# The second layer's attention and expert queries in halves of 256 tokens, with expert gathers interleaved into the second half

## The chip, the cores and the metric

The kernel runs on one core of one Trainium2 chip. The metric is the device time of one execution in microseconds (us). The core has the engines TensorE (PE; its weight loads are shown as PEld), VectorE (DVE), ScalarE (ACT), GpSimd (POOL) and SyncE (SP, which here issues weight loads and result stores), and 16 DMA engines between HBM and SBUF. Each engine runs its own instructions in program order, and the engines meet only at semaphores.

## The reference, cut to what matters

Two transformer layers over 512 tokens of width 1024, all in float32. The first layer (adaptive norm, sparse attention, latent attention, a feed-forward of width 4096) is untouched by the change. The second layer is:

```python
mod = jax.nn.silu(c) @ ada_w[l] + ada_b[l]
h = rmsnorm_2(x, norm1_g[l]) * (1.0 + sc1) + sh1
p = h @ w_in[l]
mq, mk, mv, mo, mi, mf, dq, dk, dv = jnp.split(p, split_pts, axis=-1)
qk = jax.nn.silu(causal_dwconv(jnp.concatenate([mq, mk], axis=-1), conv_w[l], conv_b[l]))
...
hm = mlstm_chunkwise(q_m, k_m, v_m, ig, lf)          # 4 heads of 128
hm = rmsnorm_2(hm, ...) * jax.nn.sigmoid(mo)
...
od = diff_attention(q_d, k_d, v_d, lam)              # 4 heads, two softmaxes each
y = jnp.concatenate([hm, od], axis=-1) @ w_out[l]
x = x + g1 * y
h2 = rmsnorm_2(x, norm2_g[l]) * (1.0 + sc2) + sh2
x = x + g2 * peer(h2, peer_w_query[l], peer_sub_keys[l], peer_u[l], peer_v[l])
return rmsnorm_2(x, final_g)
```

and the experts of it, for each block of 128 tokens:

```python
q = (xb @ w_query).reshape(TOKEN_BLOCK, P_HEADS, 2, P_HALF)
s = jnp.einsum('thpk,hpnk->thpn', q, sub_keys)
sv, si = lax.top_k(s, P_TOPK)                        # 16 of 128 keys, for each half of the key
...
fv, fpos = lax.top_k(cand, P_TOPK)                   # 16 of the 256 pairs
eidx = jnp.take_along_axis(cidx, fpos, axis=-1)
g = jax.nn.softmax(fv, axis=-1)
act = jax.nn.gelu(jnp.einsum('td,thkd->thk', xb, u_tab[eidx]), approximate=False)
return jnp.einsum('thk,thkd->td', g * act, v_tab[eidx])
```

Everything is causal in the tokens: the attention of tokens 0 to 255 needs nothing of tokens 256 to 511.

## The kernel before

Activations are kept transposed: 8 blocks of 128 features by 512 tokens (`xT`, and `hT` for the normed ones). Weights stream through two ring buffers of 2 MB each (`ring`), which SP fills: block n waits until the matmuls of block n-2 are done. A **chunk** is 128 output features, 8 accumulated matmuls of 512 tokens; PE writes it into PSUM bank j % 2, and ACT or DVE evacuates it.

The second layer runs in stages over all 512 tokens: norm `n1`; `in2a`, 17 chunks (the convolved queries and keys, the gates, values and output gates, with the four-tap convolution on DVE, L1392 and L1394); `mls`, the mLSTM attention; `dif`, the differential attention; the output projection `out2`; norm `n2`; the expert queries. The attention classes hand one **unit** (one head of one tile of 128 queries) from PE to DVE to ACT and back in a pipeline of some ten steps. A hook, `fill_pe` and `fill_dve`, puts other work into each step: the 12 chunks of `in2b` go into `mls`, half of `out2` goes into `dif`.

The expert stage has 512 **picks**: pick n is one expert slot (of 16 in each of 8 heads) for a tile of 128 tokens. One pick is

- POOL: an indirect DMA that gathers 128 rows of 8 KB, u and v of an expert for each token, into a row buffer (L1596);
- DVE: the dot product with u (L1513, `dot`);
- ACT: Gelu (L1230) and the scaling by the gate (L1231), and for an odd pick from 16 on also a diagonal matrix of the weights (L1237);
- the product with v: on DVE for even picks (L1525, `value`), on PE by that diagonal matrix for odd ones (L1072).

DVE adds the value of pick n - lag after the dot of pick n. The row buffers are the slots: 4 for the first 32 picks (lag 1), 8 after that (lag 3; four of them lie in `ring`, which is free once the weights are through). A gather waits until the slot's last value is added. Between the picks DVE chooses the experts of later heads: `pick_keys` (L1455 to L1467), `pick_pairs` (L1474 to L1479), `pick_experts` (L1485 to L1495) and `pick_gates`. The queries of tokens 0 to 255 (`pqa`) come ahead of the picks and beside the first ten; those of tokens 256 to 511 (`pqb`) are computed beside picks 10 to 30. Of each tile the sum is then scaled, added to x and normed (`last`, five steps) and stored.

## Time and profile before

| | us |
|---|---|
| median of 3 runs | 2956.39 (2953.14 to 2956.84) |
| the profiled execution, its time | 2954.73 |
| its span in the trace | 2952.6 |
| second layer's first norm (`n1`) begins | 1136.3 |
| first expert gather is issued | 1559.2 |
| eight slots in use | from 1712.8 |
| last dot product begins | 2938.3 |

PE was busy for 2285.1 us, DVE for 1711.7, ACT for 774.1 and POOL for 618.6 of the span. Busy time is that of the instructions themselves. In a row of the timeline, the bracket at the end tells how long the engine sat idle before it, and what ended that. A float32 matmul stands as two records in the trace, so a chunk of 8 matmuls has 16. The indirect DMAs move 1.05 MB each.

### The profile page before, as it was taken

The page shows a single profiled execution, that of the slowest core. Times are in us where ns is not written, and L with a number is a line of the kernel's source. Part 1 is how long each engine was busy: PE and PEld are TensorE (multiplying, and loading weights), DVE is VectorE, ACT ScalarE, POOL GpSimd, SP SyncE. Part 2 cuts the span into 40 slices and gives each one's busy share as a digit, 9 for nine tenths or more (in the row PEclk, how much of TensorE's full clock was granted, in tenths as well). Part 3 has the DMA queues.
Part 4 walks back from the last instruction along what each step waited for, and adds up shares of the span by engine and source line. Part 5 has one row for each costly group of instructions (what it writes and reads, how often), then busy time and mean ns, then how long its engine had stood idle before and what let it go on. Part 6 is the DMA issues. An engine that isn't in the chain of part 4 may idle for free.

```text
span 2952.6 us, 20335 instructions
## 1 busy us (share of the span) xinstructions
PE 2285.1 (77%) x6246; PEld 1108.0 (38%) x6246; DVE 1711.7 (58%) x3473; ACT 774.1 (26%) x2136; POOL 618.6 (21%) x540
## 2 busy tenths in 40 slices
PE   4999999999999999999977755556655565555655
PEld 2475554643444445445546621212212121121221
DVE  5422226312114324223427579999999988999987
ACT  2012332301000002222412223333333333333332
POOL 0000000000000000000002244444445444444443
PEclk8989999999999999999988977676776787768667
DMA  8520002012126520211027799999999999999997
GB/s 347 206 97 29 29 29 86 29 57 81 61 85 250 205 114 33 110 57 57 1 96 295 299 367 418 415 403 406 409 420 418 396 406 410 414 400 418 421 413 333
DMA packets 86070, 702.93 MB, mean 238 GB/s; under 512 B 9552, under 2 KB 9552, under 8 KB 10576
## 3 DMA queue, kind: packets, MB, share of 16 engines
q0 software_dynamic: 77184, 587.24, 48.9%
q1 hardware_dynamic: 7776, 106.96, 9.5%
q10 hardware_dynamic: 1008, 7.52, 0.6%
q8 instruction: 46, 0.75, 0.1%
q14 instruction: 56, 0.46, 0.0%
HBM read 699.58 MB, written 2.10 MB: 238 GB/s over the span
## 4 chain that ended last, share of the span: by engine, by line
PE 50%; DMA 22%; DVE 19%; issue 5%; POOL 2%; ACT 1%; POOLq 0%; ACTq 0%; DVEq 0%
PE PS L396 22%; DMA ring<-in_peer_uv,arena 16%; PE PS L426 8%; DMA arena<-in_peer_uv,arena 5%; DVE arena L1525 5%; PE PS L762 4%; PE PS L462 3%; DVE arena L1513 3%; PE PS L484 3%; PE PS L785 3%; DVE ring L1513 2%; PE PS L472 2%; POOL ring L1596 2%; PE PS L809 2%; PE PS L1072 1%
## 5 line engine op out<-in xcount | busy, mean ns | idle before, releaser
L1072 PE MATMUL PS<-arena 128*128 128x512 f32 x512 | 398.9, 925 | 391.3 <-ACT arena L1237 353.7
L1596 POOL DMA_INDIRECT arena<-in_peer_uv,arena x272 | 319.8, 1176 | 997.3 <-DVE arena L1495 513.3
L1072 PE MATMUL PS<-ring,arena 128*128 128x512 f32 x480 | 318.6, 804 | 156.4 <-ACT arena L1237 156.2
L1513 DVE CUSTOM_DVE_ANT_0 arena<-arena 128x1024 f32<-128x1024 f32 x272 | 327.1, 1223 | 86.3 <-DMA arena<-in_peer_uv,arena 80.8
L396 PE MATMUL PS<-arena,ring 128*128 128x512 f32 x832 | 366.0, 598 | 8.9 <-DVE arena L1322 4.8
L1072 PEld LDWEIGHTS PS<-arena 128*128 128x128 f32 x512 | 128.6, 276 | 631.8 <-ACT arena L1237 513.7
L1596 POOL DMA_INDIRECT ring<-in_peer_uv,arena x240 | 285.7, 1190 | 280.6 <-DVE arena L1525 242.7
L1513 DVE CUSTOM_DVE_ANT_0 ring<-ring,arena 128x1024 f32<-128x1024 f32 x240 | 290.6, 1228 | 48.2 <-DMA ring<-in_peer_uv,arena 47.3
L1230 ACT ACTIVATE arena<-arena 128x1 f32<-128x1 f32 x512 | 102.9, 201 | 808.3 <-DVE arena L1513 807.9
L396 PE MATMUL PS<-hT,ring 128*128 128x256 f32 (+1 forms) x944 | 308.4, 486 | 7.9 <-ACT hT L319 7.9
L1072 PEld LDWEIGHTS PS<-ring,arena 128*128 128x128 f32 x480 | 115.1, 256 | 370.4 <-ACT arena L1237 253.1
L396 PEld LDWEIGHTS PS<-arena,ring 128*128 128x128 f32 x832 | 158.4, 192 | 212.5 <-issue 195.6
L1584 POOL DMA_DIRECT2D arena<-in_ada x24 | 12.9, 539 | 1032.5 <-ACTq L292 762.2
L396 PEld LDWEIGHTS PS<-hT,ring 128*128 128x128 f32 x944 | 181.4, 194 | 127.5 <-issue 111.8
L426 PE MATMUL PS<-hT,ring 128*128 128x512 f32 x512 | 221.8, 596 | 6.5 <-ACT hT L319 6.5
L1525 DVE SCALAR_TENSOR_TENSOR arena<-arena 128x1024 f32<-128x1024 f32 x140 | 179.8, 1284 | 29.2 <-ACT arena L1231 29.2
L1231 ACT ACTIVATE arena<-arena 128x1 f32<-128x1 f32 x512 | 150.8, 295 | 16.6
L1525 DVE SCALAR_TENSOR_TENSOR arena<-ring,arena 128x1024 f32<-128x1024 f32 x120 | 154.1, 1284 | 0.1
L426 PEld LDWEIGHTS PS<-hT,ring 128*128 128x128 f32 x512 | 98.0, 192 | 130.4 <-issue 129.1
L1354 DVE SCALAR_TENSOR_TENSOR xT<-PS,modc,xT 128x512 f32<-128x512 f32 x24 | 18.0, 751 | 218.7 <-PE PS L396 218.7
L1368 DVE TENSOR_SCALAR arena<-PS 128x512 f32<-128x512 f32 x32 | 22.1, 692 | 195.7 <-PE PS L426 195.7
L566 ACT ACTIVATE arena<-arena,smalls 128x128 f32<-128x128 f32 (+3 forms) x128 | 71.7, 560 | 204.3 <-DVE smalls L564 204.3
(252 smaller groups left out, 2550.4 us busy)
## 6 DMA issues: line engine op xcount, KB each, us to landing
ring<-in_wstream SPq DMA_DIRECT2D x50, 2048.0 KB, 7.4
arena<-in_ada POOLq DMA_DIRECT2D x24, 2048.0 KB, 7.9
arena<-in_peer_uv,arena POOLq DMA_INDIRECT x272
ring<-in_peer_uv,arena POOLq DMA_INDIRECT x240, 10.1
xT<-in_xT ACTq DMA_DIRECT2D x1, 2048.0 KB, 11.3
arena<-in_alibi ACTq DMA_DIRECT2D x1, 2048.0 KB, 8.2
result<-arena SPq DMA_DIRECT2D x4, 512.0 KB, 8.0
arena<-in_subkeys ACTq DMA_DIRECT2D x1, 1024.0 KB, 4.9
```

The source lines that it names most:

```text
L396: ins = pe.matmul(o, l, r, start=(a == 0), stop=(a == len(lhs) - 1))
L426: ins = pe.matmul(bank(j % 2, n), w[:, k, m * P:(m + 1) * P], act_in(k), start=(k == 0), stop=(k == kc - 1))
L462: ins = pe.matmul(o, l, r, start=True, stop=True)
L484: ins = pe.matmul(o, l, r, start=(a == 0), stop=(a == len(pairs) - 1))
L762: ins = pe.matmul(bank(7), w[:, k, tile(j % 4)], hT[:, k, :], start=(k == 0), stop=(k == KD - 1))
L785: ins = pe.matmul(bank(5 + j % 2), lhs, rhs, start=(k == 0), stop=(k == KD - 1))
L1072: ins = pe.matmul(bank(6 + b), diag[:, k % NDIAG, :], rows[slot_of(n)][:, D + b * 512:D + (b + 1) * 512], start=opens, stop=closes)
L1230: own(act.activation(dots[:, e:e + 1], dots[:, e:e + 1], ACT.Gelu))
L1231: act.activation(wexp[:, t, e:e + 1], dots[:, e:e + 1], ACT.Copy, scale=gate[:, t, e:e + 1]).then_inc(wexp_ok, 1)
L1513: dve.tensor_tensor_reduce(u, u, h2tok[:, t % 2, :], 1.0, 0.0, ALU.mult, ALU.add, dots[:, e:e + 1]).then_inc(dot_ok, 1)
L1525: dve.scalar_tensor_tensor(out=a, in0=v, scalar=wexp[:, t, e:e + 1], in1=a, op0=ALU.mult, op1=ALU.add)\
L1596: pool.indirect_dma_start(rows[j], None, ap["peer_uv"], bass.IndirectOffsetOnAxis(ap=eidx[:, t, e:e + 1], axis=0)).then_inc(landed[j], 16)
```

## The change

- The second layer's stages run twice, as half a = 0 (tokens 0 to 255) and half a = 1 (tokens 256 to 511). Chunks have 256 columns; a weight block holds two chunks and is 1 MB (`wsecond`, 27 blocks). All 27 are loaded twice, once for each half. `in2b` and `out2` are stages of their own and no longer fill the attention's steps. The fences between the second layer's stages give way to semaphores. Convolution tails, the scans' carries, and the differential attention's keys and values of the first half are carried over; the last go through HBM (`park_kv`), and x, turned to tokens, too (`park_x`, read back when a tile is finished).
- A table of planned step times, `STAGES2`, gives for every step j of a stage the number of picks that must be done before it: `picks(a, stage, j)`. In half 0 that is up to 8, in the query stage `pq` alone. In half 1 it is 8 + 0.62 times the planned microseconds, at most 212. DVE, ACT and PE all bring their part of the picks up to that number (`Feed.to`) ahead of the same step.
- Slots: 4 for the first 16 picks (lag 1), 6 up to pick 272 (lag 2), 8 after that (lag 3).
- `pick_keys` runs once a pick over the first 14 picks of each half, for the heads 2 to 15 of it.

```diff
-EARLY = 32
-NDIAG = 4
+NDIAG = 3
+NARROW, WIDE = 16, NPICK // 2 + 16

 def slot_of(n):
-    return n % 4 if n < EARLY else n % 8
+    if n < NARROW:
+        return n % 4
+    return (n - NARROW) % 6 if n < WIDE else (n - WIDE) % 8

 def lag_of(n):
-    return 1 if n < EARLY else 3
+    return 1 if n < NARROW else 2 if n < WIDE else 3
...
+STAGES2 = [("n1", 1, 10.0), ("in2a", 17, 3.6), ("mls", 18, 2.5), ("in2b", 12, 3.6), ("dif", 26, 2.2), ("out2", 8, 3.6),
+           ("n2", 1, 14.0), ("pq", 20, 3.6), ("park", 1, 4.0)]
+EARLY_PICKS, LAST_PICK, PER_US = 8, 212, 0.62
+
+def picks(a, stage, j):
+    if a == 0:
+        return max(0, min(j - 9, (j - 5) // 2, EARLY_PICKS)) if stage == "pq" else 0
+    start = 0.0
+    for name, steps, us in STAGES2:
+        if name == stage:
+            return min(EARLY_PICKS + int(PER_US * (start + us * j)), LAST_PICK)
+        start += steps * us
...
@@ tensor
+                if a == 1:
+                    pe.wait_ge(x_parked, 32)
+                norm_pe(pe, n1, KD)
...
+                for j in range(17):
+                    values.to(picks(a, "in2a", j))
+                    if 9 <= j < 13:
+                        tokens(IN2A + j)
                     else:
+                        features(IN2A + j, h2T, (lambda k: normed(pe, n1, k)) if j == 0 else None)
...
+                mls[a].fill_pe = lambda pe, u: values.to(picks(a, "mls", u))
+                mls[a].pe(pe)
+                for j in range(12):
+                    values.to(picks(a, "in2b", j))
+                    (features(IN2B + j, h2T) if j < 8 else tokens(IN2B + j))
...
+                dif[a].fill_pe = lambda pe, u: values.to(picks(a, "dif", u))
+                dif[a].pe(pe)
+                pe.wait_ge(dif[a].tok_out, 2)
+                for j in range(8):
+                    values.to(picks(a, "out2", j))
+                    features(OUT2 + j, catT)
+                    norm_after(pe, n2, j)
...
@@ vector
+                for c in range(8):
+                    steps.to(picks(a, "in2a", c))
+                    u, dst = uT[:, c % 4, :], qhalf[:, c, :] if c < 4 else kall[:, c - 4, half(a)]
...
+                    dve.wait_ge(ev2, first + IN2A + c + 1)
...
+                steps.to(picks(a, "in2a", 12))
...
+                mls[a].fill_dve = lambda dve, u: steps.to(picks(a, "mls", u))
+                mls[a].dve(dve, own)
+                for j in range(12):
+                    steps.to(picks(a, "in2b", j))
+                dif[a].fill_dve = lambda dve, u: steps.to(picks(a, "dif", u))
+                dif[a].dve(dve, own)
+                for j in range(8):
+                    steps.to(picks(a, "out2", j))
+                    dve.wait_ge(mm2, first + OUT2 + j + 1)
+                    dve.scalar_tensor_tensor(out=xT[:, j, half(a)], in0=bank((first + OUT2 + j) % 2, HALF),
...
+                for j in range(20):
+                    steps.to(picks(a, "pq", j))
...
@@ scalar, in Attention.act and in the stages
+                    if self.fill_act is not None:
+                        self.fill_act(act, u)
...
+                for tl in range(2):
+                    act.wait_ge(x_pe, 2 * a + tl + 1)
+                    own(act.activation(xtok[:, tl, :]...))
+                    act.dma_start(park_x[2 * a + tl], xtok[:, tl, :]).then_inc(x_parked, 16)
```

How the order of work moves, at two places.

**PE in `in2a`.** Before, chunk after chunk, with nothing but the evacuation of the chunk before last to wait for (L396 is a chunk's matmul):

```order
L396 MATMUL PS<-hT,ring0 128x512 [waits evac]
L396 MATMUL PS<-hT,ring0 128x512 x7
L396 MATMUL PS<-hT,ring0 128x512 [waits evac]
L396 MATMUL PS<-hT,ring0 128x512 x7
L396 MATMUL PS<-hT,ring1 128x512 [waits evac,w_loaded1]
L396 MATMUL PS<-hT,ring1 128x512 x7
```

Now, in half 1 (L1050 is the value of an odd pick, L1080 a chunk's matmul; `diagonals` is ACT's diagonal matrix of that pick):

```order
L1050 MATMUL PS<-whole 128x512 [waits diagonals]
L1050 MATMUL PS<-whole 128x512
L1080 MATMUL PS<-whole 128x256 [waits mm2_taken,w2_loaded1]
L1080 MATMUL PS<-whole 128x256 x7
L1050 MATMUL PS<-whole 128x512 [waits diagonals]
L1050 MATMUL PS<-whole 128x512
L1080 MATMUL PS<-whole 128x256 [waits mm2_taken]
L1080 MATMUL PS<-whole 128x256 x7
```

Each chunk now stands behind the value of an odd pick, and DVE has the dot products of the next picks behind the convolution of the chunk ahead. The same place on DVE, before (L1392 and L1394 are the convolution):

```order
L1392 TENSOR_SCALAR arena<-arena,prm 128x512 [waits evac]
L1394 SCALAR_TENSOR_TENSOR arena<-arena,prm 128x512 [waits dve_own] x3
L1392 TENSOR_SCALAR arena<-arena,prm 128x512 [waits evac]
L1394 SCALAR_TENSOR_TENSOR arena<-arena,prm 128x512 [waits dve_own] x3
L1392 TENSOR_SCALAR arena<-arena,prm 128x512 [waits evac]
```

and now (L1553 is the dot product, an ISA row and a read of the accumulator; L1567 the value of an even pick; L1629 to L1638 the convolution):

```order
L1553 ISA whole<-whole 128x1024 [waits landed1]
L1553 ISA whole 128x1
L1553 ISA whole<-whole 128x1024 [waits landed2]
L1553 ISA whole 128x1
L1567 SCALAR_TENSOR_TENSOR whole<-whole 128x1024 [waits values_added_dve,expert_weights]
L1629 COPY whole<-smalls 128x3
L1636 TENSOR_SCALAR whole<-whole,prm 128x256 [waits mm2_taken,dve_own]
L1638 SCALAR_TENSOR_TENSOR whole<-whole,prm 128x256 [waits dve_own] x3
```

Two or three picks stand between two convolutions, and the convolution waits for the chunk (`mm2_taken`).

**ACT in `dif`.** Before (L566 is the exponential of a unit, L518 the copy of the turned probabilities, L522 the square root when a tile is finished):

```order
L518 ACTIVATE arena<-PS 128x512 [waits dif_summed,dif_turned]
L522 ACT_TABLE_LOAD
L522 ACTIVATE smalls<-smalls 128x4 [waits dif_ms_ready]
L566 ACT_TABLE_LOAD [waits dif_turned]
L566 ACTIVATE arena,smalls<-arena,smalls 128x512 [waits dif_weighed]
L518 ACTIVATE arena<-PS 128x512 [waits dif_summed,dif_turned]
```

Now, in half 1 (L1243 is Gelu, L1244 the scaling, L1250 the diagonal, L697 the exponential, L574 the copy of turned probabilities):

```order
L1243 ACT_TABLE_LOAD
L1243 ACTIVATE whole<-whole 128x1 [waits dots]
L1244 ACTIVATE whole<-whole 128x1 [waits act_own]
L1250 ACTIVATE whole<-cst,whole 128x128 [waits values_added_pe,expert_weights]
L697 ACT_TABLE_LOAD [waits difb_turned]
L697 ACTIVATE whole,smalls<-whole,smalls 128x512 [waits difb_weighed]
L574 ACTIVATE whole<-PS 128x512 [waits difb_summed,difb_turned]
```

Before, tables were loaded twice for each tile of 128 queries. Gelu and the exponential now alternate, and two table loads stand in every step that has a unit and a pick.

## Rows read from the trace of the kernel before


**Rows 1.** The page: the span, and busy time of each engine.

```profile
span 2952.6 us, 20335 instructions
PE 2285.1 (77%) x6246; PEld 1108.0 (38%) x6246; DVE 1711.7 (58%) x3473; ACT 774.1 (26%) x2136; POOL 618.6 (21%) x540
```

**Rows 2.** Busy time by stretch (start:end, length, engines, PEclk, DMA share, GB/s).

```profile
1150.00:1273.00 123.00, 122.31 (x282) 53.25 (x281) 35.43 (x60) 28.48 (x41) 0.00 (x0) 0.97 0.18 69
1273.00:1386.00 113.00, 109.12 (x366) 57.07 (x364) 34.28 (x101) 25.83 (x55) 0.00 (x0) 1.00 0.16 59
1386.00:1481.00 95.00, 85.87 (x384) 50.38 (x384) 43.68 (x117) 41.91 (x108) 0.00 (x0) 0.98 0.05 20
1612.00:1712.00 100.00, 81.08 (x336) 61.53 (x334) 53.87 (x101) 25.30 (x77) 28.16 (x23) 0.94 0.72 267
1800.00:2800.00 1000.00, 569.49 (x884) 205.62 (x882) 916.54 (x1908) 351.41 (x1084) 453.06 (x390) 0.74 1.00 411
```

**Rows 3.** Timeline of the last picks: three dot products and what follows one.

```profile
2920.92 1.23 DVE L1513 CUSTOM_DVE_ANT_0 arena<-arena 128x1024 f32<-128x1024 f32 x1
...
2923.39 1.23 DVE L1513 CUSTOM_DVE_ANT_0 arena<-arena 128x1024 f32<-128x1024 f32 x1 [1.24 <-DMA arena<-in_peer_uv,arena]
...
2924.54 1.28 DVE L1525 SCALAR_TENSOR_TENSOR arena<-ring,arena 128x1024 f32<-128x1024 f32 x1
2924.66 0.20 ACT L1230 ACTIVATE arena<-arena 128x1 f32<-128x1 f32 x1 [1.95 <-DVE arena L1513]
...
2925.22 0.40 ACT L1237 ACTIVATE arena<-cst,arena 128x128 f32<-128x128 f32 x1
2925.68 3.46 PE L1072 MATMUL PS<-arena 128*128 128x512 f32 x4 [1.18 <-ACT arena L1237]
2925.88 1.23 DVE L1513 CUSTOM_DVE_ANT_0 arena<-arena 128x1024 f32<-128x1024 f32 x1
```

**Rows 4.** PE's timeline beside `pqb`: values of odd picks, and two chunks of 256.

```profile
1657.50 1.98 PE L1072 MATMUL PS<-arena 128*128 128x512 f32 x4 [1.75 <-ACT arena L1237]
1659.32 7.07 PE L396 MATMUL PS<-hT,ring 128*128 128x256 f32 x32
...
1696.33 3.68 PE L1072 MATMUL PS<-arena 128*128 128x512 f32 x4 [2.75 <-ACT arena L1237]
```

**Rows 5.** DVE's timeline: three of the four taps of one convolution of 512 tokens.

```profile
1159.51 2.33 DVE L1394 SCALAR_TENSOR_TENSOR arena<-arena,prm 128x512 f32<-128x512 f32 x3
```

**Rows 6.** DVE's timeline: the first rows of one head's keys, pairs and experts, and the last.

```profile
1550.20 0.49 DVE L1455 MAX8 arena<-arena 128x8 f32<-128x128 f32 x2 [22.19 <-ACT arena L1257]
...
1552.68 0.42 DVE L1474 TENSOR_TENSOR arena<-arena 128x256 f32<-128x256 f32 x1
...
1555.74 0.17 DVE L1485 TENSOR_SCALAR arena<-arena 128x16 uint32<-128x16 uint32 x1
...
1558.70 0.17 DVE L1495 CAST arena<-arena 128x16 uint32<-128x16 f32 x1
```

**Rows 7.** Groups by line and shape: 1386 to 1481 us, and (L1230) the span.

```profile
L809 PE MATMUL PS<-arena,ring 128*128 128x512 f32 x64 | 33.0, 597 | 0.0
L566 ACT ACTIVATE arena<-arena,smalls 128x512 f32<-128x512 f32 x8 | 5.8, 720 | 13.0 <-DVE smalls L564 13.0
L518 ACT ACTIVATE arena<-PS 128x512 f32<-128x512 f32 x8 | 4.7, 582 | 3.0 <-PE PS L472 3.0
...
L1230 ACT ACT_TABLE_LOAD x34 | 43.6, 1283 | 0.9 <-DVE arena L1513 0.3
```

**Rows 8.** First chunk of the queries, first gather, and the gathers of 1555 to 1712 us.

```profile
1530.58 14.99 PE L396 MATMUL PS<-hT,ring 128*128 128x256 f32 x64
...
1559.15 0.99 POOL L1596 DMA_INDIRECT arena<-in_peer_uv,arena  x1 [513.28 <-DVE arena L1495]
...
L1596 POOL DMA_INDIRECT arena<-in_peer_uv,arena x36 | 43.4, 1206 | 623.2 <-DVE arena L1495 513.3 <-DVE arena L1525 75.7 <-PE PS L1072 20.6
```

**Rows 9.** Timeline: the last dot product.

```profile
2938.27 1.22 DVE L1513 CUSTOM_DVE_ANT_0 ring<-ring,arena 128x1024 f32<-128x1024 f32 x1 [1.19 <-DMA ring<-in_peer_uv,arena]
```

1068 lines of the change are left out of this document (575 added, 493 removed).

## The prediction

> **What bounds the kernel now.** I read the busy shares first [rows 1]. PE leads with 77%, but that is a mean over two kinds of stages, so the table by stretch is the view that counts [rows 2]. From 1150 to 1481 us, the second layer's attention, PE is busy for all but a few per cent and the DMA engines for a sixth or less. From 1800 to 2800 us, the expert picks, it is the other way round: DMA share 1.00, DVE 916.54 of 1000 us, PE 57% at a granted clock of 0.74. There 390 gathers take 1000 us, 2.56 us each; in an undisturbed stretch two picks take 4.96 us (dot products at 2920.92 and 2925.88 [rows 3]), so the DMA floor is 2.48 us a pick. DVE is close behind it: 916.54 / 390 = 2.35 us a pick. The early picks, with four slots, come at a far slower pace: 36 gathers from 1559 to 1712 us, 4.2 us each, at a DMA share of 0.72 [rows 8, 2].
>
> The idea of the change is to fill the idle DMA of the attention. What it can gain is limited by DVE, which both kinds of work need, and by the order in which three engines now meet.
>
> **Prices.** A chunk of 256 columns: 7.07 / 2 = 3.53 us [rows 4]. Dot product 1.23, value on DVE 1.28 [rows 3]. From the end of an odd pick's dot product (2924.54) to PE's start on its value (2925.68): 1.15 us. The value on PE: 1.98 us at the full clock, 3.68 where PE had been idle for 2.75 us ahead of it [rows 4]. Keys 2.5 us, pairs 3.1, experts 3.1 for a head [rows 6]. Without keys a pick costs DVE 1.23 + 1.28/2 + (3.1 + 3.1 + 0.3)/16 = 2.28 us. A convolution of 256 tokens: (0.5 + 2.33)/2 and overheads, about 1.6 us [rows 5]. A table load on ACT 1.28 us, an exponential of 512 columns 0.72 (and about 0.1 for its row sum), a copy 0.58 [rows 7].
>
> **Half 0, without picks up to its queries.** From 1136.3 us: norm 7 (half of the 14 us up to the first chunk); `in2a` 17 x 3.53 = 60; gate rows, g2 rows and decay masks 9, an estimate; `mls` 31 and `dif` 43. Those two come from `dif`'s window: 95 us less 33.0 us of fill matmuls L809 [rows 2, 7], over 42 steps, is 1.5 us a step, for 18 and 26 steps, with 4 and 5 us for finishing a tile. `in2b` 12 x 3.53 = 42, now serial; `out2` 8 x 4.0 = 32; norm 11. The queries then start at 1371 instead of 1530.6 us [rows 8]: 160 us earlier. The first keys stand 20 us after that, two heads take 18, seven early picks with a head of keys each 7 x (1.23 + 1.28 + 2.5) = 35, one more pairs and experts 6, waits 9: 88 us. DVE ends half 0 at 1459 us. Bounds: 1440 to 1475.
>
> **Half 1, 204 picks.** The point is who waits for whom.
> - Turnaround: x goes to HBM (two stores, about 8 us) ahead of PE's norm, norm 12, then picks 7 to 13 with a head of keys each, 35, and the first convolution: 59 us.
> - `in2a`, chunks 1 to 7: DVE does the picks of step c, then waits for chunk c; PE begins chunk c only after the value of the last odd pick of that same step; DVE begins step c+1 only after its convolution. So these add up. A step with two picks, odd one last: dot 1.23, value 1.28, dot 1.23, chain 1.15, PE value 1.98, chunk 3.53, evacuation 0.5, convolution 1.6 = 12.5 us, in which DMA delivers 5 picks and 2 are used. Where an even pick stands last, 2.5 us of it lie beside PE's part: 10. Steps 2 to 7 make 71 with one head's pairs, and about 1.2 us more each for PE's slower clock after its wait [rows 4]: 78. Chunk 1: 7. Together 85 us for 15 picks.
> - Rest of `in2a`: DVE runs free, 23 picks at 2.5 to 2.8 us and the gate chain: 70.
> - `mls`: a unit's weighing waits for ACT's exponential, which stands behind Gelu of the same step's picks. One pick: 1.23 + 0.12 + 0.5 + 1.28 (table) + 0.75 + 0.7 = 4.6; two: 6 to 7.5. Eight units 43; ten steps without a unit 16 picks x 2.28 and finishing, 47: 90.
> - `in2b`: DMA and slots, 28 picks x 3.0 = 85.
> - `dif`: ACT pays two table loads in each of 16 steps: 2.56 + 1.36 picks x 0.53 + 0.68 x 0.45 + 0.8 + 0.55 = 5.0 to 5.2 us: 83. Ten steps at DVE's 3.1 and finishing: 43. Together 126.
> - `out2`: the same lock as in `in2a`, with the residual for the convolution; 8 steps, 10 to 12.5 us: 95.
> - norm 18. Queries: 44 picks, two heads of DVE work, 8 blocks of 1 MB: 20 steps x 7.0 = 140.
>
> Sum 59 + 85 + 70 + 90 + 85 + 126 + 95 + 18 + 140 = 768 us, 3.8 us a pick: half 1 ends at 2227. DVE is busy for 575 of them (204 x 2.28 = 465, nine heads' keys and two heads' pairs 35, attention, norms and convolutions 75, a little over half of the 113 us in the first three stretches of rows 2); the rest is waits in the lock.
>
> **The last 300 picks.** DMA-bound as now: 286 x 2.5 = 715. The first 14 picks of this half each carry a head of keys: 14 x (2.28 + 2.5) = 67. Six slots instead of eight for 60 picks, and two tiles' `last` in the crowded part: 8. Together 790, last dot product at 3017. From there to the end of the span 14.3 us, as now (2938.27 to 2952.6) [rows 9]: 3031. The profiled execution's time lies 2.1 us over its span, and the median of the runs 1.7 us over that: **3035 us**.
>
> Against the kernel before: from 1136.3 us to the last dot product it takes 1802 us; the sum gives 323 + 768 + 790 = 1881. The gathers start 160 us sooner, but up to pick 212 they come 3.9 us apart (827 us from 1400 to 2227) in place of 2.56, which gives back more than that.
>
> **A rule of the skill against a row.** ACT's instruction after a table load starts 1.3 us after the one before the load, and the load's own row says 1283 ns [rows 7]. The Trainium skill (ScalarE: Activation LUTs, What ACT_TABLE_LOAD costs) puts a switch at about 2.66 us, a load of 1283 ns and a drain of about 1380 ns. The new order has 172 loads where 96 stood; by the skill's figure, an estimate, `dif`'s 16 steps would take 2.8 us more each and the time would be some 45 us longer. The trace shows no drain, so my sum takes 1.28.
>
> **The rivals.**
> - *The lock is loose, and half 1 runs at its busiest engine.* For it: six slots hold 15 us of gathers, DVE is never idle for long while the DMA share is 1.00 [rows 2]. DMA needs 204 x 2.48 + 26 MB of weights x 2.5 = 571, DVE 575. Then the end is 193 us earlier, 2842; with half of the waits gone, 2938. It beats the kernel before from the point where half 1 takes less than 690 us, that is if over 40% of the waits I count don't come. Against it: `mm2_taken` and `diagonals` stand in the order, and DVE has nothing else to do there.
> - *Starved slots.* Early picks with four slots took 4.2 us each [rows 8]. If six slots behave like four with the attention between a slot's use and its release, the free-running parts (95 picks) take 4.2 instead of 2.9 us: 3035 + 120 = 3155. With half of that, 3095.
> - *The same time, within 0.2%:* the gain of 160 us and the loss in half 1 cancel. It needs half 1 at 690 us.
>
> **How the numbers follow.** A measurement of this kernel can tell about 0.2%, 6 us. My forecast, 2963 to 3090: 0.70. Starved slots, over 3090: 0.13. The lock is loose, under 2950: 0.13. Within 0.2%: 0.04. The range 2950 to 3110 leaves out the loose case and the worse half of the starved one. Faster 0.13, same 0.04, slower 0.83.
>
> **What would show it.** In the changed kernel: first gather near 1400 us; PE rows of a value, then a chunk, then 4 to 7 us of idle in half 1's `in2a` and `out2`, at a granted clock clearly under 0.97; DMA share in half 1 of 0.7 to 0.8, not 1.00; DVE idle before the convolution and the residual, released by PE or ACT; table loads in each `dif` step; about 790 us from pick 212 to the last. I am wrong if DVE waits for gathers (`landed`) through half 1, which would mean DMA or the slots bound it, and wrong in size if half 0's attention without fill takes more than 1.5 us a step.

## The result

The changed kernel takes **3156.82 us** in the median of four executions (3155.16 to 3165.57), the kernel before 2956.61 beside it: a ratio of **1.068 (1.0652 to 1.0708)**. I had forecast 3035 us and a range up to 3110. The sign is right and the size is not: the loss is 200 us where I had 79.

The page of the changed kernel, where [rows 1] stood:

```profile
span 3155.4 us, 21943 instructions
PE 2339.8 (74%) x6878; PEld 1258.8 (40%) x6878; DVE 1718.7 (54%) x3546; ACT 895.5 (28%) x2308; POOL 658.0 (21%) x540
...
PEclk8989999999999999796678798778887677777876
DMA  8420111111265222245657897668899599999998
...
L1050 PE MATMUL PS<-whole 128*128 128x512 f32 x992 | 717.1, 868 | 682.9 <-ACT whole L1250 650.4
L1734 POOL DMA_INDIRECT whole<-in_peer_uv,whole x512 | 644.9, 1260 | 1440.3 <-DVE whole L1567 844.2
```

Busy times of DVE and PE are those of before within 3%: 200 us more, with nearly the same work, is waiting. The DMA row shows where. From the 18th slice (1340 us) to the 29th (2290 us) it stands at 4 to 8, with one 9 among them; nearly all 9 it is only from the 33rd (2520 us). The stages of half 1, then the last 300 picks (start:end, length, busy time of PE, PEld, DVE, ACT, POOL, PEclk, DMA share, GB/s), where [rows 2] stood:

```profile
1465.00:1500.00 35.00, 7.80 (x29) 6.19 (x27) 34.65 (x139) 8.81 (x23) 6.56 (x7) 0.60 0.60 215
1500.00:1590.00 90.00, 44.49 (x120) 27.56 (x120) 48.22 (x97) 29.12 (x61) 17.44 (x17) 0.72 0.61 222
1590.00:1704.00 114.00, 75.15 (x202) 45.85 (x203) 56.17 (x104) 53.20 (x103) 27.56 (x21) 0.77 0.68 251
1704.00:1746.00 42.00, 28.87 (x88) 14.99 (x86) 26.27 (x53) 35.04 (x64) 13.01 (x11) 0.80 0.75 276
1746.00:1888.00 142.00, 98.60 (x321) 60.95 (x321) 105.50 (x199) 44.33 (x136) 52.93 (x44) 0.90 0.91 359
1888.00:1971.00 83.00, 61.27 (x193) 30.07 (x194) 58.01 (x118) 74.61 (x137) 21.49 (x21) 0.85 0.75 285
1971.00:2036.00 65.00, 37.58 (x107) 20.34 (x108) 42.36 (x78) 21.23 (x53) 18.07 (x16) 0.72 0.70 258
2036.00:2124.00 88.00, 56.12 (x157) 35.80 (x156) 38.48 (x70) 19.28 (x53) 17.47 (x16) 0.79 0.64 239
2124.00:2324.00 200.00, 135.42 (x454) 86.20 (x454) 141.12 (x295) 65.02 (x193) 65.50 (x54) 0.87 0.83 315
2324.00:2522.00 198.00, 95.09 (x120) 30.73 (x120) 155.10 (x411) 48.49 (x158) 69.00 (x56) 0.67 0.82 316
2522.00:3141.00 619.00, 351.23 (x488) 114.94 (x488) 516.65 (x883) 209.97 (x659) 326.38 (x240) 0.75 0.99 409
```

In order: the turnaround; the eight convolutions of `in2a`; the rest of it; the units of `mls`; `mls`'s other steps with `in2b`; the units of `dif`; its end; the eight residuals of `out2`; norm and queries; picks 212 to 271; picks 272 to 511. In the second and the eighth stretch no engine is busy for two thirds of the time, and DMA neither.

One step of `in2a`, in which I had seen the lock (timeline: start, duration, engine, line, operation; the bracket is the idle time before and what ended it):

```profile
1551.15 0.35 DVE L1636 TENSOR_SCALAR whole<-whole,prm 128x256 f32<-128x256 f32 x1 [2.84 <-ACT whole L1281]
...
1552.98 1.22 DVE L1553 CUSTOM_DVE_ANT_0 whole<-whole 128x1024 f32<-128x1024 f32 x1
...
1554.12 1.22 DVE L1553 CUSTOM_DVE_ANT_0 whole<-whole 128x1024 f32<-128x1024 f32 x1
...
1554.80 0.40 ACT L1250 ACTIVATE whole<-cst,whole 128x128 f32<-128x128 f32 x1
1555.25 3.78 PE L1050 MATMUL PS<-whole 128*128 128x512 f32 x4 [4.69 <-ACT whole L1250]
...
1558.83 4.34 PE L1080 MATMUL PS<-whole 128*128 128x256 f32 x16
...
1563.27 0.39 ACT L1281 ACTIVATE whole<-PS 128x256 f32<-128x256 f32 x1 [7.35 <-PE PS L1080]
...
1563.76 0.35 DVE L1636 TENSOR_SCALAR whole<-whole,prm 128x256 f32<-128x256 f32 x1 [7.13 <-ACT whole L1281]
```

Dot product, diagonal, value, chunk, copy, convolution: one after another, 12.6 us. That is the time that I had for a step with an odd pick last (12.5), but these are picks 23 and 24, with the even one last, for which I had 10 and 1.2 for the clock. What makes up the difference is PE, which pays for its own wait. After 4.69 us of idle the value takes 3.78 us and the chunk 4.34, against 1.98 and 3.53 at the full clock, 2.6 us more and not 1.2; in this stage the granted clock is 0.72.

### Where my sum was off

By boundaries of DVE's timeline (first gather issued at 1396.5, forecast 1400):

| | forecast | measured |
|---|---|---|
| half 0 up to its last early pick | to 1459 | to about 1444 |
| turnaround, first convolutions | 59 + 85 | 146 |
| rest of `in2a` | 70 | 113 to 116 |
| `mls` and `in2b` | 175 | 185 |
| `dif` and its end | 126 | 136 to 148 |
| `out2` | 95 | 87 to 99 |
| norm and queries | 158 | 199 |
| picks 212 to 511 | 790 | 817 |

The lock that I priced (85 for the convolutions, 83 for `dif`'s units, 95 for `out2`) is there to within 8 us. What is missing is 43 us in the rest of `in2a`, of which the prediction said "DVE runs free", 41 us in the queries, 27 in the last 300 picks, and some 10 in each attention. What DVE waited for in the rest of `in2a` and in the queries (engine and line, releaser: us in total, times, longest):

```profile
DVE whole L1567 <- ACT whole L1244: 40.5, 8, 9.5
...
DVE whole L1567 <- ACT whole L1244: 29.9, 9, 5.7
DVE whole L1553 <- DMA whole<-in_peer_uv,whole: 25.5, 13, 5.0
```

The value of an even pick waits for its weight on ACT. ACT's weights of step j+1 stand behind its copy of chunk j, the chunk behind PE's value of step j's last odd pick, and with a lag of two DVE can go no further. So the same lock of three engines reaches every stage in which ACT evacuates chunks, whether DVE takes part in them or not. That was a theory from one trace; the rival was my own second one, starved slots, since its time (3155) is the one measured.

### The profile page after: what moved, and what is told of

The parts are those of the page before. It is cut to its first block and busy times, and to the rows that moved or that the text cites. A ratio compares the mean times of both kernels' runs of the same rounds, so it can differ in the third digit from the quotient of the medians.

```text
span 3155.4 us, 21943 instructions
## 1 busy us (share of the span) xinstructions
PE 2339.8 (74%) x6878; PEld 1258.8 (40%) x6878; DVE 1718.7 (54%) x3546; ACT 895.5 (28%) x2308; POOL 658.0 (21%) x540
## 3 DMA queue, kind: packets, MB, share of 16 engines
q0 software_dynamic: 77184, 587.24, 47.4%
## 5 line engine op out<-in xcount | busy, mean ns | idle before, releaser
L1050 PE MATMUL PS<-whole 128*128 128x512 f32 x992 | 717.1, 868 | 682.9 <-ACT whole L1250 650.4
L1734 POOL DMA_INDIRECT whole<-in_peer_uv,whole x512 | 644.9, 1260 | 1440.3 <-DVE whole L1567 844.2
L1553 DVE CUSTOM_DVE_ANT_0 whole<-whole 128x1024 f32<-128x1024 f32 x512 | 620.5, 1221 | 185.6 <-DMA whole<-in_peer_uv,whole 179.8
L1050 PEld LDWEIGHTS PS<-whole 128*128 128x128 f32 x992 | 232.9, 259 | 1098.5 <-ACT whole L1250 877.7
L449 PE MATMUL PS<-whole 128*128 128x512 f32 (+1 forms) x1072 | 458.9, 587 | 14.9 <-ACT whole L372 6.9
L1567 DVE SCALAR_TENSOR_TENSOR whole<-whole 128x1024 f32<-128x1024 f32 x260 | 333.3, 1282 | 79.1 <-ACT whole L1244 79.0
L1080 PE MATMUL PS<-whole 128*128 128x256 f32 x1440 | 347.2, 400 | 8.6 <-ACT whole L372 4.0
L1080 PEld LDWEIGHTS PS<-whole 128*128 128x128 f32 x1440 | 294.1, 205 | 83.5 <-issue 38.0
L1243 ACT ACTIVATE whole<-whole 128x1 f32<-128x1 f32 x512 | 102.8, 201 | 729.2 <-DVE whole L1553 727.7
L449 PEld LDWEIGHTS PS<-whole 128*128 128x128 f32 x1072 | 204.4, 192 | 260.1 <-issue 240.0
L479 PE MATMUL PS<-whole 128*128 128x512 f32 x512 | 221.9, 596 | 6.5 <-ACT whole L372 6.5
L1244 ACT ACTIVATE whole<-whole 128x1 f32<-128x1 f32 x512 | 150.8, 294 | 16.6
L479 PEld LDWEIGHTS PS<-whole 128*128 128x128 f32 x512 | 98.0, 192 | 130.4 <-issue 129.1
L538 PEld LDWEIGHTS PS<-whole 128*128 128x128 f32 x720 | 109.2, 210 | 54.7 <-issue 51.9
L516 PE MATMUL PS<-whole 64*128 64x128 f32 (+11 forms) x288 | 119.8, 501 | 5.1 <-DVE smalls L723 2.8
L837 PE MATMUL PS<-whole 128*128 128x512 f32 x256 | 122.2, 602 | 0.0
L538 PE MATMUL PS<-whole 128*128 128x64 f32 (+1 forms) x720 | 106.9, 285 | 2.3 <-DVE whole L778 1.8
L1250 ACT ACTIVATE whole<-cst,whole 128x128 f32<-128x128 f32 x248 | 99.6, 402 | 8.1
```

The source lines that it names most:

```text
L449: ins = pe.matmul(o, l, r, start=(a == 0), stop=(a == len(lhs) - 1))
L479: ins = pe.matmul(bank(j % 2, n), w[:, k, m * P:(m + 1) * P], act_in(k), start=(k == 0), stop=(k == kc - 1))
L538: ins = pe.matmul(o, l, r, start=(a == 0), stop=(a == len(pairs) - 1))
L837: ins = pe.matmul(bank(7), w[:, k, tile(j % 4)], hT[:, k, :], start=(k == 0), stop=(k == KD - 1))
L1050: ins = pe.matmul(bank(6 + b), diag[:, k % NDIAG, :], rows[slot_of(n)][:, D + b * 512:D + (b + 1) * 512], start=opens, stop=closes)
L1080: ins = pe.matmul(bank(q % 2, HALF), w[:, k, tile(c)], src[:, k, :], start=(k == 0), stop=(k == KD - 1))
```

## The experiments

In five of the kernels some of the computation is left out; their expectations say which. Before the first dot product the profiles differ by up to 20 us (it begins at 1404 to 1424 us) where the kernels are alike, so stages are compared from pick 7 on. All in us; "locked" is the changed kernel, the columns are the runs told below, and "bytes" are kernels with half of the gathered bytes:

| DVE timeline | locked | PE behind | no Gelu | both | five slots | locked, bytes | PE behind, bytes | no picks |
|---|---|---|---|---|---|---|---|---|
| 8 convolutions | 89.1 | 54.8 | 89.3 | 53.1 | 89.0 | 88.0 | 52.5 | 24.5 |
| to `mls`'s units | 116.0 | 86.0 | 92.5 | 87.2 | 116.0 | 116.0 | 73.9 | 40.2 |
| units of `mls` | 40.7 | 40.7 | 32.7 | 32.2 | 41.5 | 40.7 | 40.7 | 10.0 |
| to `dif`'s units | 143.5 | 133.8 | 144.7 | 134.9 | 160.4 | 140.2 | 119.9 | 59.1 |
| units of `dif` | 82.1 | 76.4 | 74.7 | 65.7 | 81.7 | 82.1 | 73.8 | 30.8 |
| to `out2` | 65.5 | 53.4 | 61.5 | 52.5 | 70.4 | 65.5 | 50.7 | 22.4 |
| 8 residuals | 86.5 | 47.4 | 84.0 | 47.1 | 85.0 | 86.5 | 43.6 | 26.3 |
| to pick 212 | 200.6 | 189.9 | 192.3 | 190.3 | 209.0 | 195.0 | 168.1 | |
| pick 212 to 511 | 816.9 | 814.6 | 814.2 | 817.5 | 838.4 | 690.8 | 691.0 | |

### The lock taken away: PE's values one step later

```diff
+def picks_pe(a, stage, j):
+    if a == 0:
+        return picks(a, stage, j)
+    start = 0.0
+    for name, steps, us in STAGES2:
+        if name == stage:
+            return min(EARLY_PICKS + int(PER_US * max(start + us * j - us, 0.0)), LAST_PICK)
+        start += steps * us
...
-                    values.to(picks(a, "in2a", j))
+                    values.to(picks_pe(a, "in2a", j))
```

and so in every stage of PE. Nothing else moves.

> Edit: in half 1 PE brings the values of odd picks one step later than DVE and ACT (planned time less one step of the stage), so that chunk j no longer stands behind the last odd pick of step j. Everything is computed. Lock theory (chunk behind value behind dot product, and ACT's weights behind its copy of the chunk, cost 99 us in out2, about 110 us in chunks 1 to 7 of in2a, and the waits in the rest of in2a and the queries): out2 from 99 to 60 to 75 us, in2a's convolutions 7 to 10 us apart in place of 13.8, rest of in2a and queries 20 to 60 us shorter; in all 3005 to 3080 us against 3157. Starved slots (six slots hold too little, whatever the order): odd picks now hold their slot a step longer, so no gain or up to 30 us of loss, 3150 to 3190.

**3021.02 us** (3013.43 to 3024.97), ratio to before 1.0221 (1.0198 to 1.0243): 136 us of the 200 are gone. The residuals went from 86.5 to 47.4, the convolutions from 89.1 to 54.8, and the four other stretches with chunks gained 10 to 30 us each, as the theory wants. The same kinds of step, the first two rows of the table:

```profile
1500.00:1555.00 55.00, 36.99 (x116) 24.21 (x115) 47.66 (x96) 27.92 (x60) 17.75 (x15) 0.82 0.87 330
1555.00:1640.00 85.00, 61.91 (x202) 39.48 (x201) 57.15 (x107) 53.78 (x104) 28.54 (x23) 0.89 0.90 360
```

The DMA share rose from 0.61 and 0.68 to 0.87 and 0.90, PE's clock from 0.72 and 0.77 to 0.82 and 0.89. The queries, though, gained 11 of the 41 us that I looked for. What DVE waits for now in the rest of `in2a` (1555 to 1640 us) and in the queries (1992 to 2182 us), where L1577 is the value of an even pick and L1563 the dot product:

```profile
DVE whole L1563 <- DMA whole<-in_peer_uv,whole: 20.3, 9, 5.3
...
DVE whole L1577 <- ACT whole L1254: 0.3, 1, 0.3
```

```profile
DVE whole L1563 <- DMA whole<-in_peer_uv,whole: 42.0, 24, 6.6
DVE whole L1577 <- ACT whole L1254: 2.1, 1, 2.1
```

The waits for ACT's weights, 40.5 and 29.9 us with the lock, are gone in both stages, and with that the lock in them is more than a theory. In the queries waits for gathers have grown from 25.5 to 42.0 us and taken most of their place.

### Table loads taken away

```diff
-                own(act.activation(d, d, ACT.Gelu))
+                own(act.activation(d, d, ACT.Copy))
```

> Edit: ACT does a plain copy in place of Gelu for every pick, so the experts' activation is left out of the computation, and no table is switched between Gelu and the exponential. Lock theory with 1.28 us a table load: only the steps that have a unit and a pick get shorter, dif's window from first to last weighing from 82 to 45 to 60 us, mls's from 43 to 33 to 38, the rest as it was: 3110 to 3135 us against 3157. Rival, tables cost more than their rows (2.66 us a switch, or late weights through the whole half): over 80 us, under 3080.

3105.06 us, ratio 1.0511 (1.0486 to 1.0535): 52 us less, more than I said, and not where I said. `dif` gained 7 us and not 22 to 37; the rest of `in2a`, where Silu, Sigmoid and Gelu change places, gained 23.5. What held `dif`'s units in the changed kernel, without Gelu, and then with both edits at once (L694 is the weighing of a unit, L516 its scores on PE, L1563 the dot product):

```profile
DVE whole L694 <- PE PS L516: 28.3, 7, 5.0
```

```profile
DVE whole L694 <- PE PS L516: 21.4, 7, 5.3
```

```profile
DVE whole L1563 <- DMA whole<-in_peer_uv,whole: 6.3, 4, 2.4
```

In the locked kernel DVE waits 28.3 us there for PE's scores (L516), which stand behind the values of odd picks; so the lock was in `dif` as well, beside the table loads that I had taken for all of it. ACT has 173 table loads in the changed kernel and 46 here: 127 less for 52 us is 0.4 us of the end time each, a third of a load's 1.28. A load and the Silu behind it, in the changed kernel:

```profile
1551.06 1.28 ACT L1294 ACT_TABLE_LOAD   x1
...
1552.36 0.51 ACT L1294 ACTIVATE whole<-whole,prm 128x256 f32<-128x256 f32 x1
```

The Trainium skill (ScalarE: Activation LUTs, What ACT_TABLE_LOAD costs) has about 2.66 us for a switch, 1283 ns for the load and about 1380 ns for a drain. The trace agrees with the load, 1283 ns in every row, and not with the drain: the Silu begins 0.02 us behind the load's end.

### Both

> Edit: both of the edits before, PE's values one step later and a plain copy in place of Gelu (the experts' activation is left out). Without Gelu alone dif's 16 weighings took 74 us in place of 82, with PE's values later alone 76. Theory, two bounds of nearly equal size in dif (DVE waits for PE's scores, which stand behind values; ACT is full of table loads, 73 of 77 us): the two together give far more than their sum, dif 50 to 60 us, mls from 41 to 28 to 33, and the whole run under the sum of the single gains (3157 - 136 - 52 = 2969): 2940 to 2970. Rival, the two gains overlap or DVE and DMA are next at once: dif stays over 65 us, 2970 to 3000.

2999.88 us, 1.0146 (1.0114 to 1.0178): the two gains are not even added up. `dif` fell to 65.7 us, just inside the rival's case (over 65), but the rest of `in2a` stayed at 87.2 and the last 300 picks at 817.5. With PE out of the lock, taking away tables is worth 21 us and not 52. The rival holds: something else is next at once.

### Fewer slots, fewer bytes

```diff
-    return (n - NARROW) % 6 if n < WIDE else (n - WIDE) % 8
+    return (n - NARROW) % 5 if n < WIDE else (n - WIDE) % 8
```

> Edit: five row buffers in place of six for picks 16 to 271. Everything is computed. Lock theory: the stages where PE's chunk and DVE's convolution or residual alternate (in2a chunks 1 to 7, out2) keep their times within 5 us, since two or three picks are used there in the time of four or more gathers; in2b and the 60 picks from 212 to 271 lose, together 10 to 40 us: 3167 to 3197. Starved slots: the buffers set the pace everywhere in half 1, 3.9 us a pick becomes about 4.6, 100 us or more: over 3250.

3215.84 us, 1.0853 (1.0813 to 1.0894), between the 3197 that the lock theory allowed and the 3250 of starved slots; in the profiled execution 11 us of it lie ahead of the first dot product. Convolutions, rest of `in2a`, units and residuals are unchanged within 2 us with a sixth less buffer. The loss is elsewhere: 17 us in `in2b`'s stretch, 5 and 8 ahead of `out2` and in the queries, 22 in the last 300, together 52 where I had 10 to 40. Slots are not what holds the locked stages, but in `in2b`'s stretch a slot less costs at once (DVE's waits for gathers there rise from 16.6 to 35.5 us). More than six slots in half 1 were not tried.

```diff
-                pool.indirect_dma_start(rows[j], None, ap["peer_uv"],
+                whole_row = m is None
+                pool.indirect_dma_start(rows[j] if whole_row else rows[j][:, 0:D], None, ap["peer_uv"] if whole_row else ap["peer_uv"].rearrange("n (a d) -> (n a) d", a=2),
```

> Edit: the changed kernel, and every gather after the first into a slot brings 4 KB for each of the 128 tokens in place of 8 KB, so half of the experts' data is left out. Lock theory: where PE's chunk and DVE alternate nothing changes, in2a's eight convolutions stay at 86 to 89 us and out2's eight residuals at 82 to 87, mls and dif within 3 us; only in2b, the queries and the last 300 picks get shorter, half 1 from 864 to 780 to 830. Rival, late gathers were a part of the waits in in2a and out2: these fall by 15 us or more each.

> Edit: PE's values one step later, and every gather after the first into a slot brings 4 KB for each of the 128 tokens in place of 8 KB; the other half of the row buffer keeps what was there, so half of the experts' data is left out. It halves the gathers' bytes and leaves every instruction of PE, DVE and ACT. Open: once PE is out of the lock, half 1 still takes 723 us where it would take 577 us by bytes (241 MB at 418 GB/s) and DVE is busy for 556. Theory, DMA with six slots is the bound then: chunk 0 of in2a to pick 212 from 720 to 590 to 640 us, the last 300 picks from 815 to 715 to 750 (DVE 2.35 a pick). Rival, the three engines' order still bounds it: half 1 over 680 us.

3030.09 us with the lock, 2834.36 without it. The two pairs of rows, half 1 from pick 7 to 212 and the last 300, with the lock and half of the bytes:

```profile
1477.00:2325.00 848.00, 544.13 (x1664) 327.64 (x1662) 548.74 (x1146) 349.88 (x814) 240.17 (x206) 0.81 0.49 162
2325.00:3016.00 691.00, 380.13 (x607) 129.63 (x608) 658.86 (x1293) 256.75 (x815) 383.41 (x296) 0.81 0.69 232
```

and without the lock, first with all bytes and then with half:

```profile
1466.00:2182.00 716.00, 505.72 (x1662) 314.76 (x1660) 550.80 (x1145) 351.61 (x814) 241.08 (x206) 0.84 0.88 339
```

```profile
1471.00:2128.00 657.00, 487.89 (x1664) 306.87 (x1662) 547.16 (x1147) 351.50 (x813) 244.35 (x206) 0.87 0.62 209
```

This table settles the main question. **With the lock, half of the bytes change 858 us to 848; without it, 716 to 657.** With the five slots' run beside it, starved slots don't survive that: of the changed kernel's half 1 only 10 us go with the bytes. It is also less than the 34 to 84 us that I expected from the stretches without a chunk on DVE's side, so the lock reaches further than I thought even then. Without the lock 59 us are DMA's, and the 657 that stay lie 110 over DVE's 547 busy us; I had expected at most 640. The largest of DVE's waits in these 657 us (1471 to 2128; L733 is the weighing of a unit of `mls`; "issue" is time in which DVE waited for nothing that the profile shows):

```profile
DVE whole L1563 <- DMA whole<-in_peer_uv,whole: 41.8, 25, 6.1
DVE whole L733 <- issue: 11.8, 4, 3.5
DVE whole L1577 <- ACT whole L1254: 9.4, 7, 2.5
DVE whole L733 <- ACT whole L727: 7.5, 3, 4.5
```

So it still waits for gathers, at half the bytes and a DMA share of 0.62; whether the slots, the time to landing or bursts cause that was not separated. In the last 300 picks, 691 us against the 715 to 750 expected, DVE is busy for 659 and is the bound.

### Half 1 without picks

`value`, `weight` and `pick_step` return at once, and the loop of the gathers is gone:

```diff
             def value(n):
-                if not on_pe(n):
-                    return
+                return
...
-            for n in range(NPICK):
-                t, e, j = n // NSLOT, n % NSLOT, slot_of(n)
...
```

> Edit: both halves of attention and queries as in the changed kernel, but no expert is gathered, multiplied or added (gathers, dot products, Gelu, values and the choice of later heads' experts are left out; the residual alone is normed and stored). It measures what half 1 takes without picks. All theories: half 1 from its first chunk to its last query 310 to 350 us like half 0, the whole run 1760 to 1800 us. If half 1 alone took over 400 us, something in it other than picks (fetching the weights twice, the second die of heads carried over) would be slow and part of the loss not due to the lock.

1751.76 us. That is 8 us under the range I gave. From the turnaround to its last query half 1 takes 305 us alone (granted clock 0.96), half 0 308:

```profile
1136.00:1444.00 308.00, 271.06 (x1232) 228.20 (x1231) 86.42 (x272) 82.38 (x199) 0.00 (x0) 0.88 0.29 101
1444.00:1749.00 305.00, 267.16 (x1284) 221.84 (x1284) 73.42 (x187) 86.89 (x185) 0.00 (x0) 0.96 0.29 102
```

The 305 us hold the turnaround, of which the 858 from pick 7 on leave out the first 21. Between the same two marks, ACT's second copy of x at the end of each half, it is 310 us without picks, 876 in the changed kernel (1444.3 to 2320.5) and 734 with PE behind. So a pick that is taken in half 1 costs (876 - 310) / 205 = **2.8 us in the changed kernel** and (734 - 310) / 205 = 2.1 with the lock gone. One of the last 240 costs 2.56. In the changed kernel the interleaving thus hides nothing and costs a little on top, and the gathers that start 163 us sooner are paid back in full.

### What is left: tried towards a faster kernel

All of these stand on "PE behind". The kernel before had medians of 2959 to 2963 us beside them and 2956 beside "PE behind", so a difference of some 6 us between two medians from different times says nothing by itself. First the pairs of steps in `mls` and `dif`:

```diff
         if name == stage:
+            j -= j % 2 if name in ("mls", "dif") else 0
             return min(EARLY_PICKS + int(PER_US * (start + us * j)), LAST_PICK)
...
         if name == stage:
+            if name in ("mls", "dif") and j > 0:
+                return picks(a, stage, j - 1)
```

> Edit: PE's values one step later, and in mls and dif the picks are taken every second step, so that Gelu and the exponential change places in every second step only. Everything is computed. Theory, ACT bounds dif by its table loads (2.57 us a step, 16 steps): dif from 76 to 58 to 66 us, mls from 41 to 34 to 40, 2990 to 3008 against 3021. Rival, picks in pairs make DVE and the slots wait longer (two to four picks between two units): dif and mls as long as before or longer, 3018 to 3040.

3018.24 us (3014.59 to 3024.46) against 3021: `dif`'s units 69.8, less of a gain than the theory's 58 to 66, `mls`'s 31.7, more than its 34 to 40, and the stretches behind them 7 us longer each (140.8 and 60.3). The rival's time, by another way than it said: what was saved in the units came back in the stretches behind them.

```diff
-NARROW, WIDE = 16, NPICK // 2 + 16
+NARROW, WIDE = 16, 212
```

> Edit: PE's values one step later, and eight slots with a lag of three from pick 212 instead of 272. Everything is computed. Theory: six slots with a lag of two hold a pick to 2.79 us (120 us for picks 212 to 255) where DMA could do 2.5; picks 212 to 255 take 108 to 112 us, picks 256 to 271 stay with DVE: 8 to 13 us less, 3008 to 3014 against 3021. Rival, slots do not matter there: 3018 to 3024.

3011.76 us (3003.89 to 3021.63). The last 300 picks take 795.8 in place of 814.6, of which 5 in picks 212 to 255; less than the 8 to 12 forecast there; 6 in the next 16 and 7 in the last 240 I had not expected. In my sum six slots for 60 picks stood with 8 us, together with two tiles' `last`.

```diff
-                if i < 2 * PH - 2:
+                if base == 0 and i < 2 * PH - 2:
                     pick_keys((base + 2 + i) // PH, (base + 2 + i) % PH)
                 head = base + 2 + i // PK
+                if base > 0 and i % PK == 0 and i // PK + 2 < 2 * PH:
+                    pick_keys(head // PH, head % PH)
```

> Edit: PE's values one step later, and the keys of the second half's heads 2 to 15 are chosen one head in every 16 picks (ahead of that head's pairs) in place of one at each of the picks 256 to 269. Everything is computed. Theory: those 14 picks take 5.4 us each with DVE as the bound and DMA idle, spread they lie beside DMA: 14 x (5.4 - 2.8) = 36 us less, 2980 to 2990 against 3021. Rival, DVE is so near to DMA in the last 240 picks (2.35 to 2.5 us a pick) that most comes back: 3005 to 3021.

3002.89 us (2997.78 to 3011.6). Picks 212 to 271 took 28 us less and the last 240 picks 16 us more: between theory and rival. With eight slots, keys put among DMA-bound picks are not free, for DVE has 2.35 us of work in 2.5.

```diff
-    return (n - NARROW) % 6 if n < WIDE else (n - WIDE) % 8
+    return (n - NARROW) % 6 if n < WIDE else (n - WIDE) % 10
...
-        rows = [place(70 + 8 * j, 2 * D) for j in range(6)] + [place(138 + 8 * j, 2 * D) for j in range(2)]
+        rows = [place(70 + 8 * j, 2 * D) for j in range(6)] + [place(138 + 8 * j, 2 * D) for j in range(4)]
...
+                if base > 0 and i % 4 == 0 and i // 4 < 2 * PH - 2:
+                    pick_keys((base + 2 + i // 4) // PH, (base + 2 + i // 4) % PH)
```

> Edit: PE's values one step later; from pick 212 ten slots with a lag of three (the two more lie where the queries' weights and the second half's attention operands were); the second half's keys are chosen at every fourth pick from 256 to 308. Everything is computed. With eight slots from 212 the last 300 picks took 796 us (from 815), with spread keys alone 803. Theory: with ten slots DMA runs through DVE's bursts, picks 256 to 271 take 48 to 52 us in place of 76, and the last 240 keep 605 to 612: 768 to 778 for the last 300, 2985 to 2998 us in all. Rival, DVE is the bound of the last 300 in sum (672 us busy and its own waits), so the keys' time comes back wherever it is put: 788 to 800, 3003 to 3015.

**2980.22 us**, 1.0067 (1.0043 to 1.0091), 5 us under the theory's range. The last 300 took 777 us and picks 256 to 271 took 48.8, as the theory said. But this edit changes the slots and the keys' places together. Of the 37 us less in the last 300, eight slots alone had given 19 and spread keys alone 12; what the ninth and tenth slot give by themselves is not shown.

With the pairs of steps as well:

> Edit: as the kernel with ten slots, and the picks of mls and dif taken every second step. Everything is computed. Alone, the pairs made dif 7 us and mls 9 us shorter, and the stages behind each 7 us longer. Theory (in half 1 the six slots and DMA set the pace once PE is out of the lock, so time saved on ACT is only moved): the same as with ten slots alone within 6 us. Rival, the gains add: 10 to 20 us less than it.

2985.15 us (2982.82 to 2996.49): the pairs gain nothing here either.

```diff
-NARROW, WIDE = 16, 212
+NARROW, WIDE = 16, 160
...
-EARLY_PICKS, LAST_PICK, PER_US = 8, 212, 0.62
+EARLY_PICKS, LAST_PICK, PER_US = 8, 164, 0.62
```

> Edit: as the kernel with ten slots, but half 1 takes 156 picks (to 164) in place of 204, and the ten slots begin at pick 160; 48 picks move from the second half's queries to behind them. Everything is computed. It measures the price of a pick taken in half 1 against 2.5 us for one taken later. Half 1 without picks takes about 306 us, with 204 picks 864 us in the changed kernel (2.7 us for each pick) and 723 with PE's values later (2.0). Theory, 2.0 to 2.3 us a pick in the queries: 10 to 25 us slower than with 204. Rival, the queries with 55 picks in 190 us are themselves a lock, over 2.5 us a pick: equal or up to 15 us faster.

3007.16 us (3005.73 to 3012.0), 27 us slower than with 204 picks in half 1, 2 more than the theory's most: 48 picks taken later cost 0.56 us more each, so in the queries a pick costs 2.0 us. The queries' 190 us for 55 picks are not a lock. My 158 was short of bytes: 55 gathers and 8 MB of weights, 63 x 2.5, are 158 alone, and the norm's 18 us stand ahead with three gathers in them; with half of the bytes the stretch takes 168.

```diff
-EARLY_PICKS, LAST_PICK, PER_US = 8, 212, 0.62
+EARLY_PICKS, LAST_PICK, PER_US = 8, 216, 0.65
```

> Edit: as the kernel with ten slots, with a rate of 0.65 picks a planned microsecond in place of 0.62 and up to 216 picks in half 1. Everything is computed. Theory, DMA is near its bound in half 1 (share 0.87 in the mean), a pick more there costs 2.0 to 2.5 us as later: within 6 us of it. Rival, the rate was the limit: 5 to 15 us less.

3000.07 us (2990.65 to 3003.92), 20 us slower, where I expected no change or a gain. The eight residuals took 55.0 in place of 47.3, `dif`'s units 80.3 in place of 76.5, the way from there to `out2` 49.3 in place of 53.1. So 0.62 is not too low; why the residuals with 17 picks take 8 us more than with 15 was not taken apart.

```diff
-NARROW, WIDE = 16, 212
+NARROW, WIDE = 8, 212
```

> Edit: as the kernel with ten slots, and six slots with a lag of two, and odd picks on PE, from pick 8 on in place of 16. Everything is computed. In the turnaround (picks 7 to 13, 40 us) DVE chooses a head's keys at each pick and is the bound: four values less on DVE are 5 us, two slots more hold two gathers ready. Theory: 4 to 10 us less than with ten slots alone, 2970 to 2977. Rival, PE's norm and first chunks now stand behind values: the same or up to 10 us more.

2972.34 us (2965.54 to 2985.34), 8 us less, as expected. But the ratios to the kernel before, 1.0039 (1.0023 to 1.0054) and 1.0067 (1.0043 to 1.0091), overlap, so the gain is likely and not shown.

```diff
+                if a == 1:
+                    steps.to(9)
                 norm_dve(dve, own, n1, lambda c: xT[:, c, half(a)], KD, lambda c: h2T[:, c, :], lambda c: scl[:, 16 + c:17 + c])
```

> Edit: as the kernel with ten slots and the early six (its median 2972), and DVE takes picks 7 and 8 ahead of half 1's norm n1 instead of behind it. Everything is computed. There DVE waits 10.4 us for PE's sum of squares, which waits until x is in HBM. Theory, two picks with a head of keys each, 4.8 us apiece, go into that wait: 7 to 10 us less, 2962 to 2966. Rival, DVE's part of the norm now comes later or the picks' weights are missing: the same, 2970 to 2975.

2966.23 us, 1.0026 (1.001 to 1.0041): 6 us less, with an interval that again overlaps the one before. The trace is clearer: the wait of 10.4 us for PE's sum of squares has shrunk to 1.6, and from the first dot product to the first convolution of half 1 it takes 83.6 us in place of 90.9.

```diff
-                if base > 0 and i % 4 == 0 and i // 4 < 2 * PH - 2:
-                    pick_keys((base + 2 + i // 4) // PH, (base + 2 + i // 4) % PH)
+                if base > 0 and i % 8 == 0 and i // 8 < 2 * PH - 2:
+                    pick_keys((base + 2 + i // 8) // PH, (base + 2 + i // 8) % PH)
```

> Edit: as the kernel before in this call, and the second half's keys are chosen at every eighth pick (to 360) in place of every fourth. Everything is computed. Theory, picks 272 to 311 take 2.85 us (DVE 2.28 + 2.5 / 4 = 2.9); with an eighth DVE has 2.6 and DMA 2.5: 40 picks x 0.25 = 10 us less there, and 49 picks x 0.1 = 5 us more behind them: 2957 to 2961. Rival, DVE's total is the bound of the last 300: within 3 us of the kernel with every fourth.

**2954.22 us** (2946.69 to 2967.03), against 2958.87 for the kernel before beside it: 0.9989 (0.9973 to 1.0005), no measurable difference. Against the step before it, with 1.0026 beside the same runs, it is a gain clear of noise, and 3 us better than I expected. The last 300 picks, 763 us in place of 771:

```profile
2166.00:2929.00 763.00, 447.18 (x608) 145.77 (x608) 668.59 (x1293) 258.01 (x817) 392.35 (x296) 0.72 1.00 414
```

DMA share 1.00 from end to end: 2.55 us a pick. From 3157 to 2954 everything that this idea lost was found again, but no version beat the kernel before by more than can be measured. A reason stands in the kernel without picks: the two halves take 613 us by themselves, where the kernel before reaches its first gather 423 us after the same point and has half of its queries, 57 us of chunks, beside the picks. That is some 130 us of PE and pipeline time more for attention in halves (worked out, not tried by itself), in exchange for a start of the gathers 163 us sooner.

## Why the prediction was right in its sign and wrong in its size

- **Half 0: right.** First gather at 1396.5 (1400), last early pick 15 us sooner than forecast.
- **The lock, where I placed it: right.** The convolutions took 89 us for 85, the residuals 12.4 us a step for 10 to 12.5, with the pattern of the rows and the slow clock as described; in the step shown the clock's price was twice my 1.2 us. One edit that touches nothing but PE's place in line took 136 us away, and half of the bytes took about 1 us from these stages.
- **"Rest of `in2a`: DVE runs free, 23 picks at 2.5 to 2.8 us": the step that failed.** It took 116 us. I had followed DVE's own program and found no chunk in it. I did not follow ACT's, where the copy of each chunk stands ahead of the next picks' weights. With the lock gone it is 86 (DVE's wait for ACT's weights falls from 40.5 to 0.3 us), with half of the bytes as well 74: 30 us were the lock, 12 DMA behind six slots; the 70 were below both.
- **`dif`: right time, wrong reason.** I had 5.0 to 5.2 us a step from two table loads. ACT was busy for 74.6 of 83 us, but DVE waited 28.3 us for PE's scores: two bounds, each good for most of the time. Neither edit alone gave more than 8 us, both together 16.
- **Queries: the term was mis-sized.** 158 forecast, 199 measured. 11 of the difference are the lock, and once it is gone 22 more go with half of the bytes (6 with the lock still there): DMA, which I had not made a bound there.
- **Last 300 picks: mis-sized.** 790 forecast, 817 measured: six slots and DVE's bursts cost some 20 us and not 8, and a pick in the last 240 takes 2.56 us where I put 2.5 (the row gave 2.56 for the mean, and I took the undisturbed pair).
- **Starved slots: the number of this rival came out, its mechanism did not.** It named 3155 for free stretches at 4.2 us a pick. That it met the median to 2 us is luck. The stretches came at 3.3 us a pick (44 in 143.5) and 5.0 (23 in 116), and the second, the slower, is left at 116 by five slots and by half the bytes. In the first, five slots cost 17 us and half the bytes save 3: there the slots are near to being a bound, but not what lost the time.
- **The lock is loose: wrong**, though with the lock taken out and the last picks mended half 1 takes 718 us, near the 690 that I named as the point of no loss; the kernel then ties.
- **The table load's price: right** with 1.28 us on the row; on the end time it is worth 0.4.

## What to carry to other kernels

When work is interleaved by a table of step numbers, follow each hand-over through the program order of all engines, also of the one that has time to spare: here ACT, 28% busy, carried the wait from PE to DVE. Move the consumer that no other engine's next step waits for (PE's value, on which only the release of its row buffer hangs) one step behind the others, before any number is tuned. And price interleaving by the marginal step: time of the stage with the extra work less without it, by the count, against what that work costs where it stood.
